# Moving four transposes later, and a slot mask earlier, at the end of an expert's work in a fused layer

## The reference, cut to what matters

```python
logits = xf @ w_router + b_router                  # 1024 tokens, 32 experts
top_v, top_e = lax.top_k(logits, 4)                # 4 experts for each token
gates = jax.nn.softmax(top_v, axis=-1)
...
gu = xb @ w_gu[e] + b_gu[e]                        # (tokens of e, 1024) @ (1024, 2048)
gate, up = gu[:, :1024], gu[:, 1024:]
gate = jnp.minimum(gate, 7.0); up = jnp.clip(up, -7.0, 7.0)
h = (up + 1.0) * gate * jax.nn.sigmoid(1.702 * gate)
y = h @ w_down[e] + b_down[e]                      # (tokens of e, 1024) @ (1024, 1024)
y * gate_of_token                                  # added up over the 4 experts
```

## Time and profile before

| | |
|---|---|
| median of 3 runs | 2655.09 us (2654.3 to 2655.69) |
| the profiled execution | 2654.3 us, its span 2652.5 us |
| PE busy | 2466.4 us (93%) |
| DVE busy | 1757.0 us (66%) |
| ACT busy | 1390.5 us (52%) |
| POOL busy | 357.1 us (13%) |
| HBM traffic | 189 GB/s over the span |

### The profile page before, as it was taken

The page is one execution under the profiler, slowest core; times in us unless marked ns, Lnnn a source line. Parts: engine busy times, 40 slices in busy tenths (PEclk is TensorE's granted clock), DMA queues, the critical chain, the costliest instruction groups (busy, mean ns, idle before and its releaser), DMA issues.

```text
span 2652.5 us, 37894 instructions
## 1 busy us (share of the span) xinstructions
PE 2466.4 (93%) x11204; PEld 1773.2 (67%) x11205; DVE 1757.0 (66%) x2804; ACT 1390.5 (52%) x2029; POOL 357.1 (13%) x233
## 2 busy tenths in 40 slices
PE   7999997898995799999999999999999999999990
PEld 3544457577452577777777777777777777777770
DVE  0386866455235556678967599577959869558596
ACT  0368614554111344556746477456747657446472
POOL 0002821100200110101101021011101101001012
PEclk9999989799995899999999999999999999999995
DMA  4100020002004455577968599586959959657584
GB/s 158 64 4 32 0 111 1 1 1 84 5 34 165 177 178 180 200 268 257 346 237 285 184 326 331 190 286 221 332 191 346 318 175 372 198 187 272 191 308 149
DMA packets 81644, 488.48 MB, mean 184 GB/s; under 512 B 13683, under 2 KB 14963, under 8 KB 30454
## 3 DMA queue, kind: packets, MB, share of 16 engines
q1 hardware_dynamic: 66512, 449.67, 46.5%
q0 software_dynamic: 13104, 34.11, 5.9%
q10 hardware_dynamic: 1974, 4.02, 0.5%
HBM read 465.42 MB, written 36.70 MB: 189 GB/s over the span
## 4 chain that ended last, share of the span: by engine, by line
PE 70%; DVE 16%; issue 7%; ACT 3%; DMA 2%; DVEq 2%; POOL 0%; POOLq 0%; ACTq 0%; SPq 0%
PE ps L777 14%; PE ps L779 13%; PE ps L778 13%; DVE wlo L1560 10%; PE ps L523 7%; PE ps L534 5%; PE ps L702 4%; PE ps L798 3%; PE ps L684 2%; PE ps L665 1%; PE ps L808 1%; PE ps L672 1%; PE ps L552 1%; PE ps L764 1%; DVE gu L1577 1%
## 5 line engine op out<-in xcount | busy, mean ns | idle before, releaser
L1560 DVE TENSOR_TENSOR wlo<-raw,whi 128x1024 fp32r<-128x1024 f32 x776 | 932.6, 1221 | 273.8 <-ACT whi L1065 254.5
L1065 ACT ACTIVATE whi<-raw 128x1024 fp32r<-128x1024 f32 x776 | 817.7, 1059 | 440.8 <-PE ps L779 407.7
L777 PE MATMUL ps<-whi,xhi 128*128 128x512 f32 x1440 | 582.5, 404 | 0.0
L778 PE MATMUL ps<-wlo,xhi 128*128 128x512 f32 x1440 | 563.8, 392 | 0.0
L779 PE MATMUL ps<-whi,xlo 128*128 128x512 f32 x1440 | 561.8, 390 | 0.0
L777 PEld LDWEIGHTS ps<-whi,xhi 128*128 128x128 f32 x1440 | 270.3, 188 | 93.2 <-issue 40.1
L779 PEld LDWEIGHTS ps<-whi,xlo 128*128 128x128 f32 x1440 | 270.7, 188 | 59.0
L778 PEld LDWEIGHTS ps<-wlo,xhi 128*128 128x128 f32 x1440 | 270.9, 188 | 50.3
L777 PE MATMUL ps<-whi,hhi 128*128 128x512 f32 x720 | 299.0, 415 | 0.0
L1728 POOL DMA_INDIRECT acc<-ysb,idx_cur x45 | 131.1, 2912 | 1236.5 <-ACT ysb L1113 1232.5
L779 PE MATMUL ps<-whi,hlo 128*128 128x512 f32 x720 | 283.0, 393 | 0.0
(11 more groups left out here) (312 smaller groups left out, 2673.6 us busy)
## 6 DMA issues: line engine op xcount, KB each, us to landing
raw<-in_w_gu SPq DMA_DIRECT2D x260, 1024.0 KB, 6.8
raw<-in_w_dn SPq DMA_DIRECT2D x128, 1024.0 KB, 5.9
xT<-in_xT SPq DMA_DIRECT2D x2, 2048.0 KB, 15.7
raw<-in_w_out SPq DMA_DIRECT2D x2, 2048.0 KB, 10.0
h1all<-in_x SPq DMA_DIRECT2D x4, 1024.0 KB, 8.3
hext<-h1all SPq DMA_DIRECT2D x8, 512.0 KB, 11.6
acc<-accst SPq DMA_DIRECT2D x8, 512.0 KB, 2.6
fin<-acc SPq DMA_DIRECT2D x2, 2048.0 KB, 13.3
```

The costliest lines, as they stand in the source:

```text
L777: pe.matmul(bank_ap, hi, whi[:, slot, col, :], start=start, stop=False)
L778: pe.matmul(bank_ap, hi, wlo[:, slot, col, :], start=False, stop=False)
L1065: act.activation(whi[:, j % 2, 2 * g:2 * g + 2, :], raw[:, (j + 2) % 3, 2 * g:2 * g + 2, :], ACT.Copy)\
L1560: dve.tensor_tensor(wlo[:, j % 2, s, :], raw[:, (j + 2) % 3, s, :], whi[:, j % 2, s, :].bitcast(f32), ALU.subtract).then_inc(lo_done, 1)
```

## The change

On PE the `x` transposes move later: `x` 0 comes after `down` 2 and 3 in place of 2, `x` 1 after 4 and 5, `x` 2 after 6 and `x` 3 after 7, as the last work of the item. ACT's and DVE's orders follow. On DVE `mark_slots`, which was the last work of an item, now stands right behind the low part of `h` 3. The added wait of PE ahead of `down(6, 7)` is for the same event for which `turn` of `x` 1, two lines above, has already waited.

```diff
                 pe.wait_ge(tr_free[1], fill_of(i, "h", 1))
-                down(range(2, 3), i, n1, blocks)
+                down(range(2, 4), i, n1, blocks)
 
                 pe.wait_ge(tokens_in, i + 2)
                 turn(xg, (1, 0), 0, fill_of(i, "x", 0))
-                down(range(3, 4), i, n1, blocks)
+                down(range(4, 6), i, n1, blocks)
                 turn(xg, (1, 0), 1, fill_of(i, "x", 1))
-                down(range(4, 5), i, n1, blocks)
+                pe.wait_ge(tr_free[1], fill_of(i, "h", 3))
+                down(range(6, 7), i, n1, blocks)
                 turn(xg, (1, 0), 2, fill_of(i, "x", 2))
-                down(range(5, 6), i, n1, blocks)
+                down(range(7, 8), i, n1, blocks)
                 turn(xg, (1, 0), 3, fill_of(i, "x", 3))
-                down(range(6, 8), i, n1, blocks)
...
                 turned_hi(hhi, 3, fill_of(i, "h", 3), len(blocks))
-                take_hi(6, (2,), i)
+                take_hi(6, (2, 3), i)
                 turned_hi(xhi, 0, fill_of(i, "x", 0))
-                take_hi(6, (3,), i)
+                take_hi(7, (0, 1), i)
                 turned_hi(xhi, 1, fill_of(i, "x", 1))
-                take_hi(7, (0,), i)
+                take_hi(7, (2,), i)
                 turned_hi(xhi, 2, fill_of(i, "x", 2))
-                take_hi(7, (1,), i)
+                take_hi(7, (3,), i)
                 turned_hi(xhi, 3, fill_of(i, "x", 3))
-                take_hi(7, (2, 3), i)
...
                 turned_lo(hhi, hlo, 3, fill_of(i, "h", 3, 0), len(blocks))
-                take_lo(6, (2,), i)
+                mark_slots(ex, i + 2, i + 3)
+                take_lo(6, (2, 3), i)
                 turned_lo(xhi, xlo, 0, fill_of(i, "x", 0, 0))
-                take_lo(6, (3,), i)
+                take_lo(7, (0, 1), i)
                 turned_lo(xhi, xlo, 1, fill_of(i, "x", 1, 0))
-                take_lo(7, (0,), i)
+                take_lo(7, (2,), i)
                 turned_lo(xhi, xlo, 2, fill_of(i, "x", 2, 0))
-                take_lo(7, (1,), i)
+                take_lo(7, (3,), i)
                 turned_lo(xhi, xlo, 3, fill_of(i, "x", 3, 0))
-                take_lo(7, (2, 3), i)
-                mark_slots(ex, i + 2, i + 3)
```

## The result

The changed kernel takes 2741.65 us (median, 2736.57 to 2743.91) against 2654.7 us (2653.18 to 2655.69) for the kernel before on the same chip: a ratio of 1.0324 with an interval of [1.0311, 1.0337], 87 us slower. Its profiled execution is the fastest of all of its 15 executions: 2728.7 us, with a span of 2726.9 us and a mean granted clock of 0.952. The other 14 took 2736.6 to 2744.2 us at 0.945 to 0.949.

What follows compares the result with a forecast made beforehand. Double items were held bound by PE, single ones by a nearly full DVE with PE stalling. Single items 49.5, last item 1, doubles minus 1 and clock 22 made 71 us on 2654.3: 2726 as median, range 2695 to 2748.

Steps and rivals of the forecast that it cites:

- The likeliest case: Whole kernel: late waits, an uncovered loop end and a lowered clock give 2726 us, own range 2708 to 2745; chance 0.64.
- the clock: PE's granted clock falls after a single item's idle time: 1.2 us each, 22 us in all, bounds 0 and 31.
- the single items' loss: Each of 18 single items with an item after it grows by 2.75 us, 49.5 us in all.
- The waits: In a single item PE waits for DVE's low parts: 0.35 us at x 2 and 1.05 us at x 3.
- The chain of DVE operations: From h 3's low part DVE runs mask, weight pieces and x low parts; x 1 is seen at 1299.58.
- The bare loop end: Behind a single item's x 3 little is queued, so the next bias matmul starts 2.8 us later; PE idles 2.45.
- The sequencer runs past the wait: Rival: PE's loop end stays hidden, leaving 0.5 us per single item, about 2665 us; chance 0.10.
- The clock holds: Rival: the loop end shows but PE's clock doesn't fall, dropping 22 us, 2704 us; chance 0.15.
- Double items: Their loop end stays hidden by 0.4 us or so; they still take 73.7 to 73.9 us.
- the rival that doubles suffer by their own loop end: Cover in 13 double items falls short, 0.4 us plus at worst 1.7 each, up to 2753 us; chance 0.03.
- Faster: Rival: x 1's low part is ready when PE reaches x 3, saving 16.5 us, 2638 us; chance 0.08.
- old stalls: Before the change PE waits 0.27 us at h 3 and 0.60 at x 1, 0.87 us a single item.

Runs made afterwards that it cites:

- experiment 1: The changed kernel with mark_slots back as the last work of DVE's item, the x transposes still late: 2686.09 us, ratio 1.0117.
- experiment 2: The kernel before with only mark_slots moved behind the low part of h 3, old transpose order: 2684.03 us, ratio 1.0107.
- experiment 5: The kernel before with mark_slots moved behind the low part of x 2, old transpose order: 2634.48 us, ratio 0.991.
- experiment 7: The changed kernel's late transposes with mark_slots moved behind the low part of x 2: 2670.33 us, ratio 1.0062.
- experiment 6: The kernel before with mark_slots behind the low part of x 2, plus x 3 moved behind down 6 and 7: 2636.4 us, ratio 0.9933.
- experiment 4: The changed kernel plus two unused float32 products of constants on PE behind x 3 of each single item: 2704.46 us, ratio 1.019.
- experiment 3: The changed kernel plus five unused float32 products of constants on PE behind x 3 of each single item: 2743.92 us, ratio 1.0325.
- experiment 8: The changed kernel with x 3 ahead of down 7 in place of behind it: 2713.96 us, ratio 1.023.

## Why the prediction was right, step by step

Both moved things in all the places tried, in us (medians):

| | mask at the end | behind `h` 3 | behind `x` 2 |
|---|---|---|---|
| `x` transposes as before | 2655 | 2684 | 2634 |
| `x` transposes late | 2686 | 2742 | 2670 |

The two moves don't add up: 31 us for the transposes alone, 29 for the mask alone, and 87 together.

**The total.** 2726 was forecast with 2695 to 2748; 2741.65 came. The likeliest case with its own range (2708 to 2745) is the one that happened, 16 us short, and nearly all of this is one term, the clock. The other misses nearly cancel: the single items' loss is 46 us for 49.5, and the first two items add 5.5 us that were in no term. That 2741.65 lies inside the case's own range is partly luck: the terms that the prediction names for it reach to 2739 at most (2704, 31 for the clock, 4 for a DVE that starts later), and its 2745 has no working. The single items take 41.6 to 43.4 us, where 42 to 44 were forecast.

**The waits.** Forecast 0.35 us at `x` 2 and 1.05 at `x` 3; measured 0.4 to 0.6 and about 1.0. The chain of DVE operations is the forecast one, back to back. That the mask stands in it is shown by experiments 1, 2, 5 and 7: with it elsewhere no wait of PE for a low part of `x` is left in a single item, with it alone there are 2 us of it.

**The bare loop end.** Forecast 2.8 us from `x` 3's start to the bias matmul; measured 2.37 to 2.79. L872 shows at 1309.3 with `x` 3 at 1309.31, as the earlier trace rows had it for `down(2)`. Together with the waits a single item grew by 2.3 to 2.7 us at full clock (forecast 2.75), 46 us for 18 of them (forecast 49.5).

**The sequencer runs past the wait (rival, about 2665).** It fell, in the profile after and in experiment 6: where the last wait is open early L872 comes 3.2 us ahead of `x` 3, where it opens late L872 comes with it. The Trainium skill ("Perfetto Trace Analysis", Tensor Engine Instruction) says of matmuls and weight loads that one waits in a queue of its own while the next is fetched, which would have given this rival's time; at these waits the traces don't show it. The line of the transposes' waits, L795, has 65 steps of the sequencer itself in the trace before (EVENT_SEMAPHORE), so at least part of these waits are not carried by a matmul, and the section may simply not be about them; no run tells which.

**The clock.** The mis-sized term: 22 us forecast, 37 measured by experiment 4 against the changed kernel, and some 30 in the profiled execution. Its upper bound, 18 times 1.7, was too low as well, for two reasons. The price of one fall isn't bounded by the single one that the trace before showed: the low level lasted twice as long three times and then cost 2.9 to 3.1 us. And the number and length of falls differ from one execution to the next (0.945 to 0.952 on average), where I had only one execution of a kernel with hardly any. Why one execution of the same kernel is granted less than another stays open. The price of the one fall in the earlier trace rows was read rightly, but with a slip on the way: twice 2.86 us is 5.7 and not 5.6, which would give 6.0 us and not 5.9; the same bias matmul and 24 others do take 5.9 us where the clock holds (1108.08 to 1113.97, the fourth item of the kernel before).

**The clock holds (rival, 2704).** It fell, since 16 of 18 ends are followed by the lower level. Its time is what experiment 4 gives when the clock is made to hold, 2704.46. That the two agree to 1 us is luck in part: the single items' loss was 3.5 us less than forecast, and the first two items made up for it.

**The first item, not foreseen.** Its end costs more than the others:

```profile
959.72 0.60 PE L808 MATMUL ps<-brow,cb 3*128 3x512 bf16 x1 [4.90 <-issue]
```

Where 1.89 us stood before, it is 4.90 now. I had counted this end among those that cost nothing new. Wherever `x` 3 goes late this end is as long (4.9 to 5.2 us idle in experiments 1, 3, 4, 7 and 8); in experiment 6, where it goes last but its wait is passed early, it is 2.2. It is the first pass through the loop only; what takes the sequencer so long there no run tells apart. The first item is 4.7 us longer in all (80.5 for 75.8); the other 1.7 us stand at its start, where the clock is still low from the stretch ahead of the loop. The first 5 us of the item, in the changed kernel and then in the one before:

```profile
879.19:884.19 5.00, 5.00 (x14) 3.69 (x15) 0.64 (x1) 0.00 (x0) 0.00 (x0) 0.61 0.08 33
882.92:887.92 5.00, 5.00 (x21) 3.94 (x22) 0.10 (x1) 0.00 (x0) 0.00 (x0) 1.00 0.01 3
```

This isn't the change's doing: the profiles of experiments 1, 4, 5, 6 and 7 have it too, those of 2, 3 and 8 don't.

**Double items.** Forecast 73.7 to 73.9, measured 73.82 behind a double item and 73.76 behind a single one where the clock holds. Where it falls behind a single one, the double item is 75.4 to 76.8 us long; this is the single item's price, paid in the next. So the rival that doubles suffer by their own loop end (2753) fell.

**Faster (rival, 2638).** It asked for the low part of `x` 1 when PE comes to `x` 3. Experiment 7 gives all that the mask can give and still has 2 us bare an item. The 16.5 us of old stalls that this rival wanted to win are real, but they are won by moving the mask with the transposes left alone (experiment 5: 21 us), not by moving the transposes.

## What to carry to other kernels

Ahead of a loop's end ask not which instruction stands last on an engine but when the last wait of its program is passed; the work that the engine still has before it at that moment hides branches and table loads (2.7 us here), and work that is done by then hides nothing. An operation that nobody waits for soon belongs behind the low parts or copies that another engine does wait for soon and ahead of work for which its own engine would wait, and not, as before this change, behind everything. Price an idle stretch of PE of 2 us at the stretch and again at the clock behind it, here 1.4 to 3.1 us for each fall; less where idle time follows that the slower matmuls can fill (0.8 us in experiment 8).

## What the runs showed of the hardware, unexpected

- One wait of 2 us in the middle of a stream of matmuls brought the granted clock to its lower level in 10 of the 19 single items (experiment 2). I had thought that only the item's end, with its two pieces, would.
- What a fall of the clock costs depends on what follows: 13 falls in experiment 8, with idle time right behind the slower matmuls, cost some 0.8 us each, the 16 in the changed kernel 1.4 to 3.1 us.
- A float32 product of 512 columns that isn't split into halves took 0.88 us, as two recorded matmuls of 0.44 (experiment 3), where one matmul on a split half takes 0.23.
- Executions of the changed kernel spread over 15 us (2728.7 to 2744.2), and the mean granted clock with them (0.952 to 0.945); so one profile can be off by half a per cent where the clock falls often.
